# Attention stage of a two-layer hybrid block: the four lx pairs ahead of the four r pairs, where they took turns

## The reference, cut to what matters

```
p = h @ w_in[l]                      # split into gla q,k,v,r | att q,k,v | lru x,y | gates
gla_out = rms_norm(o) * silu(r)      # r: 1024 columns
s = q @ k.T * HEAD_DIM ** -0.5       # 8 query heads, 2 key/value heads, after per-head RMSNorm and rotary
att_out = softmax(s) @ v
xc = depthwise_conv(lx, 4 taps)      # lx: 1024 columns; then gates, scan, output of the RG-LRU branch
```

## Time and profile before

| what | value |
| --- | --- |
| median of three runs | 2046.06 us (2041.23 to 2046.12) |
| the profiled execution's own time | 2039.92 us |
| its span (first to last instruction) | 2038.2 us |
| mean granted TensorE clock | 0.985 of full speed |
| TensorE busy | 1945.4 us, 95% of the span |
| VectorE busy | 1164.4 us, 57% |
| ScalarE busy | 1002.7 us, 49% |

### The profile page before, as it was taken

The page is one execution under the profiler, slowest core; times in us unless marked ns, Lnnn a source line. Parts: engine busy times, 40 slices in busy tenths (PEclk is TensorE's granted clock), DMA queues, the critical chain, the costliest instruction groups (busy, mean ns, idle before and its releaser), DMA issues.

```text
span 2038.2 us, 26205 instructions
## 1 busy us (share of the span) xinstructions
PE 1945.4 (95%) x10784; PEld 1578.9 (77%) x10784; DVE 1164.4 (57%) x1622; ACT 1002.7 (49%) x1413; POOL 24.3 (1%) x57
## 2 busy tenths in 40 slices
PE   5999999999999999899999999799898999989998
PEld 3788777777777768577766787688687888989997
DVE  3565445545555334765555433766555678668874
ACT  4533346545654223543333333644355688566663
POOL 2000000000000000000000000000000000000000
PEclk9999999999999999899999999899999999999999
DMA  8211111122233554145454533121222354545553
GB/s 310 66 55 53 57 55 60 62 78 93 93 95 103 186 183 148 52 135 199 163 198 163 176 104 106 52 73 55 75 84 72 125 161 147 173 145 166 185 180 122
DMA packets 67990, 244.96 MB, mean 120 GB/s; under 512 B 7696, under 2 KB 8736, under 8 KB 67872
## 3 DMA queue, kind: packets, MB, share of 16 engines
q1 hardware_dynamic: 64736, 232.81, 34.6%
q0 software_dynamic: 1696, 5.24, 0.8%
q10 hardware_dynamic: 1440, 5.24, 0.7%
HBM read 242.21 MB, written 1.05 MB: 119 GB/s over the span
## 4 chain that ended last, share of the span: by engine, by line
PE 73%; DVE 15%; ACT 5%; DMA 3%; issue 3%; SPq 0%; ACTq 0%; DVEq 0%
PE ps L1454 52%; PE ps L1444 4%; DVE wlo L833 4%; PE ps L1389 3%; DVE fa L862 2%; DMA wada<-in_w_ada 2%; ACT whi L438 2%; PE ps L1489 2%; PE ps L1706 2%; PE ps L1796 2%; PE ps L1727 1%; DVE state L1177 1%; DMA wraw<-in_weights 1%; PE ps L1620 1%; PE ps L1630 1%
## 5 line engine op out<-in xcount | busy, mean ns | idle before, releaser
L833 DVE TENSOR_TENSOR wlo<-wraw,whi 128x1024 fp32r<-128x1024 f32 x352 | 429.5, 1223 | 403.4 <-ACT whi L438 402.5
L438 ACT ACTIVATE whi<-wraw 128x1024 fp32r<-128x1024 f32 x352 | 371.4, 1056 | 377.9 <-PE ps L1454 193.7
L1454 PE MATMUL ps<-hh,whi 128*128 128x512 f32 (+1 forms) x1664 | 381.2, 351 | 1.9 <-ACT l_ti L772 1.8
L1454 PE MATMUL ps<-hl,whi 128*128 128x512 f32 (+1 forms) x1664 | 375.0, 348 | 0.0
L1454 PE MATMUL ps<-hh,wlo 128*128 128x512 f32 (+1 forms) x1664 | 344.0, 348 | 1.9 <-DVE wlo L833 1.9
L1454 PEld LDWEIGHTS ps<-hh,whi 128*128 128x128 f32 x1664 | 274.5, 191 | 58.7 <-issue 22.6
L1454 PEld LDWEIGHTS ps<-hl,whi 128*128 128x128 f32 x1664 | 277.1, 191 | 40.2 <-issue 3.6
L1454 PEld LDWEIGHTS ps<-hh,wlo 128*128 128x128 f32 x1664 | 269.6, 190 | 40.4 <-issue 3.0
L862 DVE SCALAR_TENSOR_TENSOR fa<-ps,par,fa 128x510 f32<-128x510 f32 (+1 forms) x176 | 100.1, 610 | 27.8 <-ACT fa L516 26.2
L1454 PE MATMUL ps<-bh,whi 128*128 128x512 f32 (+1 forms) x384 | 89.3, 354 | 0.0
L1454 PE MATMUL ps<-bl,whi 128*128 128x512 f32 (+1 forms) x384 | 82.2, 336 | 0.0
(11 more groups left out here) (285 smaller groups left out, 2556.6 us busy)
## 6 DMA issues: line engine op xcount, KB each, us to landing
wraw<-in_weights SPq DMA_DIRECT2D x352, 512.0 KB, 3.5
wada<-in_w_ada SPq DMA_DIRECT2D x80, 512.0 KB, 5.0
ada_first<-in_w_ada ACTq DMA_DIRECT2D x10, 512.0 KB, 16.6
wgate<-in_w_gate POOLq DMA_DIRECT2D x16, 256.0 KB, 2.8
ada_first<-in_w_ada SPq DMA_DIRECT2D x6, 512.0 KB, 23.9
x<-in_xt SPq DMA_DIRECT2D x4, 512.0 KB, 9.9
out_x<-x SPq DMA_DIRECT2D x4, 256.0 KB, 2.2
par<-in_params POOLq DMA_DIRECT2D x1, 370.0 KB, 8.0
```

The source lines that it names most:

```text
L438: A_(whi[u % HI][:], wraw[RING_W[u] % RAW][:], ACT.Copy).then_inc(s_hi, 1)
L833: V.tensor_tensor(wlo[s][:], wraw[s][:], whi[u % HI][:].bitcast(F32), ALU.subtract).then_inc(s_lo, 1)
L1454: ins = mm(dst[:, r, c:], w[:, kk, r * P:(r + 1) * P], x_[:, UK * h + kk, c:], start=h == 0 and k in (0, 2) and kk == 0, stop=h == m - 1 a ...
```

## The change

Only the list of pairs changes. Before, `r` and `lx` took turns (`r` 0, `lx` 0, `r` 1, `lx` 1, ...); now `lx` 0 to 3 come first and `r` 0 to 3 behind them. Units 28 to 35 are then `lx` and units 36 to 43 `r`. The weights are laid out in the new order. No instruction of the computation is added or removed, and the lists written out by hand stay as they are; which pair is taken at which edge follows from the list (the table below), and so does the bank pair of each.

```diff
 PAIR_ORDER = ([("gqk", 0), ("gqk", 1), ("gv", 0), ("gqk", 2), ("gv", 1), ("gqk", 3), ("gv", 2), ("akv", 0), ("gv", 3),
-               ("akv", 1)] + [("aq", i) for i in range(4)] + [(n, i) for i in range(4) for n in ("r", "lx")]
+               ("akv", 1)] + [("aq", i) for i in range(4)] + [(n, i) for n in ("lx", "r") for i in range(4)]
                + [(n, i) for i in range(4) for n in ("g1", "b1")]
```

## The result

| what | before | after |
| --- | --- | --- |
| median of the first comparison (5 runs each) | 2044.42 us | 2033.34 us |
| ratio of it, 95% interval | | 0.9945 (0.9931 to 0.9960) |
| second comparison, other runs (18 and 8) | 2041.74 us | 2034.73 us |
| ratio of it, 95% interval | | 0.9966 (0.9956 to 0.9977) |
| the profiled execution's own time | 2039.92 us | 2032.88 us |

The account below looks back on a forecast made before the run. TensorE, busy 1945.4 of 2038.2 us, was taken as the bound. 0.9 + 2.6 + 1.5 = 5.0 us made 2039.9 into 2034.9 profiled, or 2041.1 against the median of 2046.06; range 2035 to 2047.

Parts of the forecast that it names:

- The sum of 5.0 us: Whole kernel: 0.9 for head 4 of layer 0, 2.6 and 1.5 for head 3 of layer 1.
- the dip of head 5: Layer 1: 3.3 us at half clock (1.2 GHz) behind head 5's wait of 1.97 us, forecast to stay.
- the dip of head 3: Layer 1: 3.0 us at half clock behind head 3's wait, forecast to go, a gain of 1.5 us.
- the swap of head 5: Layer 1, TensorE ahead of head 5's `tile_swap`: the prediction gave it no term.
- Head 4 of layer 0: Edge 34: TensorE's wait for the `Square` falls from 2.75 to 1.85 us, a gain of 0.9.
- Head 3 of layer 1: Edge 32: wide parts cut TensorE's wait before `tile_swap` from 4.46 to 1.85 us, a gain of 2.6.
- The thin covers: VectorE in time by 0.2 us at layer 0 head 4's transposes, by 0.1 to 0.3 at layer 1's `tile_rope`.
- hidden anyway: Rival, chance 0.12: gain returns as later waits or thin covers fail slightly; less than 2 us left, 2045.
- the wait moves: Rival, chance 0.09: late VectorE makes TensorE wait at head 3's scores in layer 1; about 4 us slower, 2050.
- a rival with 0.20: Both dips go, chance 0.20: layer 1's half clock behind head 5 goes too, 1.65 us more, gain 6.6, 2039.4.
- had no dip: Layer 0's wait of 2.75 us amid wide parts kept full clock, so head 3's 1.85 in layer 1 would too.
- Nothing is gained or lost there: Layer 1, the heads other than head 3: covers hold and head 5's wait stays, so no gain or loss.

Follow-up runs that it names:

- e4: Old order with a Copy in place of the Silu on r, so the stages have no table load; 0.9982 of the kernel before.
- e8: New order with the Silu table loaded ahead of the lx pairs of edges 30 and 34; 2038.20 us, 0.9986 of before.
- e11: New order in layer 0, layer 1 in the order r, lx, lx, r, lx, lx, r, r; 2035.77 us, 0.9975 of before.
- e2: New order in layer 1 only, old order in layer 0; 0.9967 of the kernel before.
- e5: The changed kernel run again, unedited; 2034.73 us, 0.9966 of the kernel before.
- e1: The kernel before (old order) run again, unchanged; 0.9992 of before.
- e9: Old order with idle TensorE products in layer 1, 24 ahead of head 3's swap, 14 ahead of head 5's column sums; 0.9993 of before.
- e10: New order with idle TensorE products in layer 1, 13 ahead of head 3's swap, 14 ahead of head 5's column sums; 0.9962 of before.
- e3: New order in layer 0 only, old order in layer 1; 0.9989 of the kernel before.
- e7: New order in layer 0, layer 1 in the order r, lx, lx, lx, lx, r, r, r; 2033.12 us.
- e12: e6 with 13 idle TensorE products ahead of the swap of head 3 in layer 1; 0.9948 of the kernel before.
- e6: e7 with layer 0 in the order lx, lx, lx, r, lx, r, r, r besides; 2030.13 us, 0.9942 of the kernel before.

## Why the prediction was right or wrong

The sum of 5.0 us was too small by three of its terms, all of layer 1: the dip of head 5, taken to stay; the dip of head 3, taken at 1.5 us; and the swap of head 5, taken at nothing.

**Right, in mechanism and size: the waits.** Head 4 of layer 0 was to wait 1.85 us and waits 1.75. Head 3 of layer 1 was to wait 1.85 and waits 1.83, by the wide parts: e4 without table loads keeps the 4.46, and e8 and e11 with them have 1.83. The thin covers held, and e8 shows how thin one is. Table loads: 8, as counted. Nothing moved into a new wait, and the cases "hidden anyway" and "the wait moves" did not come.

**Wrong: that "the 1.97 us of head 5" stay "with their dip".** The wait stayed and the dip did not, in the three profiles of the new order without added loads (first, e2, e5). It was there in all four of the old order with unfilled waits and in e8. I had this as a rival with 0.20. Nothing in head 5's own work differs in length up to the wait; what differs is when it comes, and what lies ahead of it, the longer wait of head 3 with its half clock above all. The table loads alone do not decide it, since e4 has none in the stage and has the dip. Why the old order met the dip each time and the new order did not is open.

**Right, but for a reason that does not hold: the dip of head 3 goes.** The reason was that a wait amid wide parts "had no dip". In e1 and e9 the clock fell behind that same wait of 2.75 us in layer 0, in e4, e5 and e10 behind the one of 2.02 us in head 5 of layer 0, and in e11 behind the wait of 1.83 us in head 3 itself. One profile had stood for the rule; that the term came out was luck as far as the reason goes.

**Mis-sized: "cost half of that, 1.5".** The term for head 3's dip came from one execution. Of four profiles of the old order two have 3.4 us at half clock there and two have 6.7 or 6.8, in which TensorE works for 5.5 us. Together with head 5, the clock cost the old order's stage 2.7 us by e9, net of a wait that the slow clock hid.

**Missing: the swap of head 5.** "Nothing is gained or lost there" overlooked that, with the clock up, the two table loads ahead of `tile_norm` make TensorE wait 0.91 us in the old order (e9); in the new order that chain has no loads. The first `wgate` product's 0.2 us went too.

**The sum with the measured terms.** Layer 1's stage was 135.1 us on average of four and is 128.4 on average of three: 6.7 us in place of 4.1. By parts: 4.46 - 1.83 = 2.6 for head 3, 0.9 for the swap of head 5, 0.2 at the first gates, 2.7 for the clock, 6.4 in all. Layer 0 gives 1.0. That is 7.7 us. The rest of the kernel gives 0 to 1.5 more: behind the stage it takes 428.1 to 428.3 us in every profile with layer 1 in the new order, and 429.7 to 429.8 in two of the old order's plain profiles (first, e3), 428.3 in e1, by a wait for `wlo` of 1.9 or 0.4 us. In the profiles with 0.4 the clock has fallen some 15 us earlier, behind the wait for `l_ti`, and the slow products cover most of the wait; in those with 1.9 it falls behind the `wlo` wait itself, or in e4 not at all. Both kinds occur among the old orders and among the mixed ones (e7 and e12 have 1.9, e6 has 0.4), so this part cannot be put down to the change for certain. So 7.7 to 9.2, between the two measurements of 7.0 and 11.1, whose intervals overlap from 8.2 to 9.2.

**The range.** Its low end, 2035, was the forecast of 2041.1 less two dips of 1.65 and some 3 us for the lower runs. It needed the spread of the clock's loss, which one profile cannot show; the 5 us between the runs of before were the sign of it, and I used them for the chances only. Faster by over 0.3% had 0.37.

## What to carry to other kernels

Where independent pieces of matrix work are spread beside a chain of small steps, put the long pieces beside the long chains: the wait is the chain's length less the work beside it, and can be worked out from a timeline, here to 0.2 us. Keep activations that need another function table behind the last one that needs the loaded one. And count a wait of TensorE as possibly more than its length: behind 6.4 us of waits the half clock cost 2.7 us more here, and where it falls differs between executions, so its price is to be taken from several profiles.

## What the runs showed of the hardware

The waits of TensorE repeat from execution to execution to 0.02 us (4.46, 4.46, 4.45, 4.46 before the swap of head 3 in four profiles), while stretches at 1.2 GHz behind the same waits come, go and double in length; the runs of the old order beside the experiments spread by 6.0 to 9.4 us, with the mean clock between 0.982 and 0.986. A wait of 1.97 or 1.98 us amid 256-column products had the half clock behind it in five of eight profiles. A wait of 1.83 us amid 512-column products had it in one of seven (e11; not in the first profile of the new order, e2, e5, e6, e7 and e8). Filling the waits of heads 3 and 5 with idle products kept the clock at 1.00 at both in e9, where all four unfilled profiles of the old order had it fall; in e10 and e12 it had not fallen unfilled either.
